# Loading the expert weights of a hybrid diffusion layer in blocks of 512 rows instead of 256

## The chip, the cores and the metric

One NeuronCore of a Trainium2 chip runs the whole program. The metric is the device time of one execution, in microseconds (us). TensorE (PE) multiplies, VectorE (DVE) and ScalarE (ACT) work element by element, GpSimd (POOL) here only sets buffers to zero and issues small transfers, and SyncE (SP) issues the weight transfers. Every transfer between HBM and the on-chip memory is spread over the core's 16 DMA engines.

## What is computed

One layer of a diffusion backbone runs on two groups of 128 tokens with 1024 features each, in float32: a modulated RMSNorm, a token mixer (attention, a gated recurrence and a gated MLP behind one input projection), an output projection, and then a mixture of experts in which each of the 256 tokens uses 4 of 32 experts. The part that the change touches is the last one:

```python
def swiglu_expert(xb, wg, bg, wu, bu, wd, bd):
    gate = jnp.minimum(xb @ wg + bg, SWIGLU_LIMIT)
    up = jnp.clip(xb @ wu + bu, -SWIGLU_LIMIT, SWIGLU_LIMIT)
    glu = gate * jax.nn.sigmoid(SWIGLU_ALPHA * gate)
    return ((up + 1.0) * glu) @ wd + bd

# routed_moe: logits = hf @ wr + br; gates = softmax of the top 4;
# out[token] += gate * swiglu_expert(hf[token]) for each of its 4 experts
```

Each expert has three 1024 x 1024 float32 matrices of 4 MB, so the 32 experts are 384 MB of weights, and every one of them is read once. The other weights are 41 MB.

## The kernel before

All weights pass through one buffer, `ring`, of 12 slots of 1 MB (8 KB in each of 128 partitions). SP issues one transfer for a slot, in a fixed order, one after another, with a counter `n`: 8 of `w_mod` (n = 0 to 7), 13 of `w_in`, 12 of `w_mod`, 4 of `w_out`, 4 of `w_mod`, and from n = `AT_MOE` = 41 on the 384 of the experts. Transfer n goes to slot n mod 12, and `slot_free` makes SP wait until PE has used up chunk n - 12. PE counts used chunks in the semaphore `chunks_used`, and waits for the semaphore of a slot (`slot_wait`) before it reads it.

The rows of the 1 MB differ in how they lie in HBM. A partition of a `w_mod` slot receives four separate runs of 2 KB, one of a `w_in` slot eight runs of 1 KB, one of a `w_out` slot two of 4 KB. An expert's chunk is 256 whole rows of a matrix; partition p takes rows 2p and 2p + 1, which are neighbours in HBM, so it is one run of 8 KB:

```python
return sp.dma_start(view.rearrange("p (k n) -> p k n", k=2),
                    w[0, bass.ds(e, 1), 256 * r:256 * (r + 1), :].rearrange("a (p k) n -> p (a k) n", p=P))
```

Since a partition holds two neighbouring rows of the matrix, the other operand has to be ordered in the same way. That is why DVE writes the normalised tokens in a permuted order of features (`pairs`, `rows_out_of`, line 951; the last step in line 959), why the router's weights `rw` are loaded with the same permutation, and why the activated products `ab` are written permuted (line 1038).

The order of PE's work in the expert stage is written out by hand (line 1524 on): the gate product of expert 0, then for each expert e the UP product, `combine` of expert e - 1 (its result is added to the tokens, line 1482), the GATE product of e + 1, the transposes of the activations of e (line 1495), the `gather` of the tokens of e + 2 (line 1447), the DOWN product of e, and the transposes of its gates (line 1502). A product is 4 chunks of 8 matmuls (line 1471), and after each chunk `chunks_used` rises by one. UP and GATE products begin with 4 matmuls for the bias (line 1466). The weights are loaded in the order GATE 0, UP 0, GATE 1, DOWN 0, UP 1, GATE 2, DOWN 1 and so on, to UP 31 and DOWN 31. Each group of 3 matrices for one expert is 12 chunks, a full ring.

Beside PE, DVE clips the gate product (line 1025) and the UP product (line 1033) and multiplies them (line 1038), and ACT copies tokens, transposed activations and results (lines 618, 626, 630). Loops for experts with more than 64 tokens follow; they are compiled in but are not entered with these inputs. The last step is a second RMSNorm and four output transfers.

Of the kernel before, what the change touches and what calls it, by code (L numbers as in the profile page):

```python
# [20 lines left out]
ALU = mybir.AluOpType  # L21
# [3 lines left out]
P = 128  # L25
# [33 lines left out]
AT_MOE = AT_MODG2 + 4  # L59
AT_END = AT_MOE + 12 * NE  # L60
WOUT = [2, 3, 0, 1]
# [39 lines left out]
def hybrid_layer(nc, x_prompt, x_sample, cache_k, cache_v, state_hgrn_fwd, state_hgrn_bwd, c, c_ctx,  # L101
# [6 lines left out]
    with ctx:  # L108
# [178 lines left out]
        def at_moe(m, e):  # L287


            return AT_MOE + 12 * e + {GATE: 0 if e == 0 else -4, UP: 4, DOWN: 12 if e + 1 < NE else 8}[m]  # L290

# [22 lines left out]
        def _(sp):  # L314
# [36 lines left out]
            def load_rows(view, w, e, r):  # L351
                return sp.dma_start(view.rearrange("p (k n) -> p k n", k=2),  # L352
                                    w[0, bass.ds(e, 1), 256 * r:256 * (r + 1), :].rearrange("a (p k) n -> p (a k) n", p=P))

            def load_matrix(m, e):
                nonlocal n
                assert n == at_moe(m, e)
                for r in range(4):
                    slot_free(n)
                    load_rows(ring[:, n % RING, :], (w_gate, w_up, w_down)[m], e, r).then_inc(slot_loaded[n % RING], 16)  # L360
                    n += 1
# [10 lines left out]
            with sp.If(n_over > 0):  # L372
                with sp.Fori(0, MAX_OVER) as j:
                    with sp.If(n_over > j):
                        e = sp.value_load(small_i[0:1, bass.ds(j, 1)], min_val=0, max_val=NE - 1)
                        sp.wait_ge(chunks_used, j * 12 + AT_END)
                        for cidx in range(12):
                            load_rows(ring[:, cidx, :], (w_gate, w_up, w_down)[cidx // 4], e, cidx % 4).then_inc(ev("over_loaded"), 16)

# [8 lines left out]
        def _(pool):  # L388
# [27 lines left out]
            small_load("mixer_loaded", ong, bcast_row(hgrn_onorm_g[0:1, :]))  # L416
            small_load("mixer_loaded", rw.rearrange("p (r k) e -> p r k e", r=4), router_w[0].rearrange("(r p k) e -> p r k e", p=P, k=2))
            small_load("mixer_loaded", rbias, router_b)
# [34 lines left out]
        def _(act):  # L453
# [182 lines left out]
            for e in range(NE):  # L636
                act_transposed(e)
                if e + 1 < NE:
                    sigmoid_step(e + 1)
                if e + 2 < NE:  # L640
                    tokens_out(e + 2, e % 2)
                rows_out(e, at_moe(DOWN, e) + 4)
            act.wait_ge(ev("over_list"), 1)
            n_over = act.value_load(small_i[0:1, 16:17], min_val=0, max_val=MAX_OVER)
            with act.If(n_over > 0):
                with act.Fori(0, MAX_OVER) as j:
                    with act.If(n_over > j):
                        tokens_out(j + NE, 0)
                        sigmoid_step(j + NE)
                        act_transposed(j + NE)  # L650
                        rows_out(j + NE, j * 12 + AT_END + 12)

# [11 lines left out]
        def _(dve):  # L664
# [266 lines left out]
            def pairs(ap):  # L931
                return ap.rearrange("p (r m k) -> p r m k", r=4, k=2)

            def rows_out_of(t):
                return rows[:, t, :].rearrange("p (r k m) -> p r m k", r=4, k=2)

# [16 lines left out]
            for t in range(2):  # L953
                dve.wait_ge(ev("rms2"), t + 1)
                ch.step(V.reciprocal(rs2[:, t:t + 1], rs2[:, t:t + 1]))
                dve.wait_ge(ev("rows_scaled"), t + 3)
                for r in range(4):
                    block_r = rows[:, t, 256 * r:256 * (r + 1)]
                    ins = V.scalar_tensor_tensor(block_r, block_r, rs2[:, t:t + 1],
                                                 shf[:, 256 * r:256 * (r + 1)].rearrange("p (m k) -> p k m", k=2), ALU.mult, ALU.add)  # L960
                ins.then_inc(ev("h2_ready"), 1)
# [69 lines left out]
            def up_step(count, done):  # L1031
                dve.wait_ge(chunks_used, done)
                V.tensor_scalar(upb, B[1], -LIMIT, LIMIT, ALU.max, ALU.min).then_inc(ev("up_clip"), 1)  # L1033
                dve.wait_ge(ev("glu_ready"), count + 1)
                dve.wait_ge(ev("up_clip"), count + 1)
                for r in range(2):
                    cols = slice(256 * r, 256 * (r + 1))
                    ins = V.scalar_tensor_tensor(ab[:, cols].rearrange("p (k m) -> p m k", k=2), upb[:, cols].rearrange("p (m k) -> p m k", k=2), 1.0,  # L1038
                                                 actb[:, cols].rearrange("p (m k) -> p m k", k=2), ALU.add, ALU.mult)
                ins.then_inc(ev("a_ready"), 1)  # L1040

# [14 lines left out]
            pick_tokens(1)  # L1056
            gate_step(0, at_moe(GATE, 0) + 4, later=False)
            for e in range(NE):
                if e + 2 < NE:
                    dve.wait_ge(ev("xe_ps"), e + 2)  # L1060
                    pick_tokens(e + 2)
                if e:
                    dve.wait_ge(ev("gT_ps"), e)
                pick_gates(e)
                glu_step(e)
                up_step(e, at_moe(UP, e) + 4)
                if e + 1 < NE:
                    gate_step(e + 1, at_moe(GATE, e + 1) + 4)
                gates_out(e)
            dve.wait_ge(ev("over_list"), 1)  # L1070
            n_over = dve.value_load(small_i[0:1, 16:17], min_val=0, max_val=MAX_OVER)
            with dve.If(n_over > 0):
                with dve.Fori(0, MAX_OVER) as j:
                    with dve.If(n_over > j):
# [13 lines left out]
                        ins.then_inc(ev("pg_ready"), 1)  # L1088
                        gate_step(j + NE, j * 12 + AT_END + 4)
                        glu_step(j + NE)  # L1090
                        up_step(j + NE, j * 12 + AT_END + 8)
                        gates_out(j + NE)
# [19 lines left out]
        def _(pe):  # L1112
# [338 lines left out]
            def main_rows(m, e, r):  # L1451

                n = at_moe(m, e) + r
                slot_wait(n)
                return ring[:, n % RING, :]

            def over_rows(m, e, r):
                return ring[:, 4 * m + r, :]

            def product(bank, m, e, lhsT, arrived, pick=None):  # L1460


                if m < 2:
                    row = ident[:, NE * (m + 1) + e:NE * (m + 1) + e + 1].to_broadcast([P, CAP]) if pick is None else pick
                    for half in range(2):
                        mm(bank[CAP * half:CAP * (half + 1), :], row, mbias[:, 512 * half:512 * (half + 1)], start=True, stop=False)  # L1466
                for r in range(4):
                    w = arrived(m, e, r).rearrange("p (k n) -> p k n", k=2)
                    for kk in range(2):
                        for half in range(2):  # L1470
                            ins = mm(bank[CAP * half:CAP * (half + 1), :], lhsT(2 * r + kk), w[:, kk, 512 * half:512 * (half + 1)],  # L1471
                                     start=m == 2 and r == 0 and kk == 0, stop=r == 3 and kk == 1)
                    ins.then_inc(chunks_used, 1)
# [74 lines left out]
            with pe.If(n_over > 0):  # L1548
                with pe.Fori(0, MAX_OVER) as j:
                    with pe.If(n_over > j):  # L1550
                        gather(j + NE)
                        pe.wait_ge(ev("xe_ready"), j + (NE + 1))
                        pe.wait_ge(ev("over_loaded"), j * 192 + 192)
                        product(B[0], GATE, 0, tokens(0), over_rows, over_pick[:, 0, :])
# [35 lines left out]
```

## Time and profile before

| | |
|---|---|
| median of 3 runs | 1229.23 us (1227.69 to 1230.12) |
| the profiled execution | 1229.05 us |
| its span, from the first to the last instruction | 1227.2 us |
| around the span | 1.85 us |
| PE busy | 1178.6 us, 96% of the span |
| DVE, ACT, POOL busy | 21%, 12%, 2% |
| moved by DMA | 456.00 MB, mean 372 GB/s |
| expert stage, from the first GATE product on | 264.5 us to 1212 us of the span |

A busy time of 96% says little here by itself, because matmuls are pipelined and an engine can be busy while it is late. What is to be read is which wait ends last in each part of the expert stage, and how fast the DMA engines move the weights there. All times below count from the start of the span.

### The profile page before, as it was taken

Reading aid. Unit: us, or ns where it says so; the run is one execution under the profiler, and the core shown is the slowest. Engines: PE = TensorE matmul, PEld = TensorE weight load, DVE = VectorE, ACT = ScalarE, POOL = GpSimd, SP = SyncE. Lnnn points to the kernel's source line nnn. Section 1 sums busy time; section 2 is a strip of 40 time slices with the busy share of each in tenths; the row PEclk is TensorE's granted clock in tenths of the full one; section 3 lists DMA queues with packets and bytes.
Section 4 is the critical chain, followed back from the end, with each engine's and each line's share of the span. In section 5 each row is a group of like instructions: output and inputs, shape, how many; then the busy total and the mean of one; then the engine's idle time right before and its main releaser. Section 6 shows DMA issues by size and latency. Waiting matters only on the chain.

```text
span 1227.2 us, 13618 instructions
## 1 busy us (share of the span) xinstructions
PE 1178.6 (96%) x5974; PEld 546.0 (44%) x5974; DVE 256.9 (21%) x567; ACT 142.9 (12%) x273; POOL 20.2 (2%) x39
## 2 busy tenths in 40 slices
PE   6599999999999999999999999999999999999995
PEld 1288975464444444444444444444443333333321
DVE  1325574421111111111111111111111111111113
ACT  1122423111000000000000100000000000000001
POOL 3100000000000000000000000000000000000000
PEclk9599999999999999999999999999999999999998
DMA  9993439639999999999999999999999999999993
GB/s 319 331 362 120 153 122 394 250 127 398 383 422 421 421 421 421 421 422 421 420 421 421 422 420 421 421 421 421 421 421 421 422 420 421 420 422 422 419 422 113
DMA packets 86051, 456.00 MB, mean 372 GB/s; under 512 B 7968, under 2 KB 21300, under 8 KB 36711
## 3 DMA queue, kind: packets, MB, share of 16 engines
q1 hardware_dynamic: 82928, 446.73, 90.1%
q0 software_dynamic: 2064, 6.98, 1.7%
q10 hardware_dynamic: 998, 1.40, 0.5%
q8 instruction: 48, 0.79, 0.3%
q14 instruction: 13, 0.10, 0.0%
HBM read 453.38 MB, written 1.70 MB: 371 GB/s over the span
## 4 chain that ended last, share of the span: by engine, by line
PE 60%; DMA 22%; DVE 2%; SPq 1%; issue 0%; ACT 0%; DVEq 0%
PE bank L1471 39%; DMA ring<-in_w_up 22%; PE bank L1447 7%; PE bank L1466 4%; PE bank L1482 4%; PE bank L1347 2%; PE bank L1495 1%; PE bank L1142 1%; PE bank L1502 1%; SPq L352 1%; PE bank L1174 0%; PE bank L1149 0%; PE bank L1415 0%; PE bank L1511 0%; PE bank L1383 0%
## 5 line engine op out<-in xcount | busy, mean ns | idle before, releaser
L1471 PE MATMUL bank<-ring,at_pool 128*64 128x512 f32 x2048 | 456.7, 595 | 5.6 <-DMA ring<-in_w_up 4.5
L1471 PEld LDWEIGHTS bank<-ring,at_pool 128*64 128x64 f32 x2048 | 145.7, 137 | 306.1 <-issue 270.3
L1471 PE MATMUL bank<-ring,k_pool 128*64 128x512 f32 x1024 | 227.5, 596 | 2.6 <-ACT k_pool L626 1.4
L1471 PEld LDWEIGHTS bank<-ring,k_pool 128*64 128x64 f32 x1024 | 70.3, 137 | 134.1 <-issue 125.0
L1447 PE MATMUL bank<-d_pool,rows 128*128 128x64 f32 x1024 | 118.0, 273 | 0.0
L1447 PEld LDWEIGHTS bank<-d_pool,rows 128*128 128x128 f32 x1024 | 116.9, 192 | 1.3 <-issue 1.3
L626 ACT COPY k_pool<-bank 128x512 f32<-128x512 f32 x32 | 18.7, 585 | 579.0 <-PE bank L1495 579.0
L1019 DVE COPY cumT<-bank 128x256 f32<-128x256 f32 x32 | 13.6, 424 | 346.2 <-PE bank L1502 346.2
L1025 DVE TENSOR_SCALAR k_pool<-bank 128x512 f32<-128x512 f32 x32 | 22.1, 691 | 256.5 <-PE bank L1471 256.5
L1466 PE MATMUL bank<-kv_pool,cst 128*64 128x512 f32 x256 | 69.4, 620 | 0.7 <-DVE small_i L1054 0.7
L1482 PE MATMUL bank<-d_pool,cumT 64*128 64x512 f32 x256 | 63.6, 615 | 0.6 <-DVE cumT L1019 0.6
L1033 DVE TENSOR_SCALAR k_pool<-bank 128x512 f32<-128x512 f32 x32 | 22.1, 691 | 199.7 <-PE bank L1471 199.7
L1192 PE MATMUL bank<-colsT,ring 128*128 128x256 f32 x224 | 52.2, 395 | 0.8 <-DVE colsT L729 0.8
L1192 PEld LDWEIGHTS bank<-colsT,ring 128*128 128x128 f32 x224 | 44.2, 199 | 8.1 <-DVE colsT L729 1.2
L1195 PE MATMUL bank<-ring,colsT 128*128 128x256 f32 x192 | 43.4, 380 | 0.0
L630 ACT COPY d_pool<-bank 128x512 f32<-128x512 f32 x32 | 18.7, 585 | 209.1 <-PE bank L1471 209.1
L1482 PEld LDWEIGHTS bank<-d_pool,cumT 64*128 64x128 f32 x256 | 22.1, 186 | 41.0 <-issue 40.2
L1142 PE MATMUL bank<-ring,condT 128*32 128x512 f32 x192 | 29.5, 749 | 10.6 <-DMA ring<-in_w_mod 10.6
L1195 PEld LDWEIGHTS bank<-ring,colsT 128*128 128x128 f32 x192 | 35.7, 190 | 4.6
L1038 DVE SCALAR_TENSOR_TENSOR kv_pool<-k_pool 128x256 f32<-128x256 f32 x64 | 33.9, 611 | 3.3
L618 ACT COPY at_pool<-bank 128x512 f32<-128x512 f32 x32 | 18.7, 585 | 91.4 <-PE bank L1447 91.4
L1347 PE MATMUL bank<-ring,colsT 128*128 128x512 f32 x64 | 27.9, 593 | 0.0
(295 smaller groups left out, 544.4 us busy)
## 6 DMA issues: line engine op xcount, KB each, us to landing
ring<-in_w_gate SPq DMA_DIRECT2D x128, 1024.0 KB, 20.5
ring<-in_w_up SPq DMA_DIRECT2D x128, 1024.0 KB, 21.4
ring<-in_w_down SPq DMA_DIRECT2D x128, 1024.0 KB, 20.7
ring<-in_w_mod SPq DMA_DIRECT2D x24, 1024.0 KB, 9.4
ring<-in_w_in SPq DMA_DIRECT2D x13, 1024.0 KB, 12.5
ring<-in_w_out SPq DMA_DIRECT2D x4, 1024.0 KB, 6.9
k_pool<-in_const_masks POOLq DMA_DIRECT2D x1, 1024.0 KB, 7.9
g<-in_b_mod POOLq DMA_DIRECT2D x2, 512.0 KB, 12.2
```

The source lines that it names most:

```text
L618: nc.scalar.copy(xe[:, buf].rearrange("p k s -> p (k s)"), B[3]).then_inc(ev("xe_ready"), 1)
L1025: V.tensor_scalar(actb, B[0], LIMIT, None, ALU.min).then_inc(ev("gate_min"), 1)
L1033: V.tensor_scalar(upb, B[1], -LIMIT, LIMIT, ALU.max, ALU.min).then_inc(ev("up_clip"), 1)
L1038: ins = V.scalar_tensor_tensor(ab[:, cols].rearrange("p (k m) -> p m k", k=2), upb[:, cols].rearrange("p (m k) -> p m k", k=2), 1.0, actb[ ...
L1142: ins = mm(B[mod_bank(n)][32 * j:32 * (j + 1), :], condT[:, 4 * r + j, :], w[:, j, :], start=r == 0, stop=r == 1, tile_position=(0, 32 * j))
L1192: ins = mm(bank[:, 256 * r:256 * (r + 1)], w[:, k, P * r:P * (r + 1)], hT[:, k, :, :], start=k == 0, stop=k == KT - 1)
L1195: ins = mm(bank[:, 256 * r:256 * (r + 1)], hT[:, k, r, :], w[:, k, :], start=k == 0, stop=k == KT - 1)
L1347: ins = mm(B[2 * t + half], catT[:, 2 * WOUT[i] + kk, t, :], w[:, kk, 512 * half:512 * (half + 1)], start=i == 0 and kk == 0, stop=i == 3 ...
L1447: ins = mm(B[3][:, CAP * k:CAP * (k + 1)], rows[:, t, P * k:P * (k + 1)], Ptok[:, t, :], start=t == 0, stop=t == 1)
L1466: mm(bank[CAP * half:CAP * (half + 1), :], row, mbias[:, 512 * half:512 * (half + 1)], start=True, stop=False)
L1471: ins = mm(bank[CAP * half:CAP * (half + 1), :], lhsT(2 * r + kk), w[:, kk, 512 * half:512 * (half + 1)], start=m == 2 and r == 0 and kk = ...
L1482: ins = mm(B[4 + 2 * t + half], gT[r, P * t:P * (t + 1)], ysb[r, :], start=False, stop=False)
```

## The change

A transfer now brings 512 rows of an expert's matrix (2 MB) into two neighbouring slots, and partition p takes rows 4p to 4p + 3, one run of 16 KB. The ring is used as `PAIRS` = 6 pairs of slots in this stage; the first pair is the one that `pair_of` gives for n = 41, which is slots 6 and 7. A product has 2 such chunks of 16 matmuls, and PE waits and counts once for each. SP waits for a pair as a whole: for the first six transfers until the last earlier chunk in either of its two slots is used, after that until the transfer six before is used. The permutations of the tokens, of the router's weights and of the activated products go from two to four neighbouring rows. In line 959 there are now 2 instructions over 512 columns for each token block where there were 4 over 256, and in line 1038 there is 1 over 512 for each expert where there were 2 over 256. Everything before n = 41 is loaded as it was.

```diff
+PAIRS = RING // 2
+AT_END = AT_MOE + 6 * NE
...
-            return AT_MOE + 12 * e + {GATE: 0 if e == 0 else -4, UP: 4, DOWN: 12 if e + 1 < NE else 8}[m]
+            return AT_MOE + 6 * e + {GATE: 0 if e == 0 else -2, UP: 2, DOWN: 6 if e + 1 < NE else 4}[m]
+
+        def pair_of(n):
+            return (n - AT_MOE + 3) % PAIRS
+
+        def pair_loaded(n):
+            return slot_loaded[2 * pair_of(n)]
+
+        def pair_loads(n):
+            before = len(range(2 * pair_of(n), AT_MOE, RING))
+            return 16 * (before + (n - AT_MOE) // PAIRS + 1)
+
+        def pair_rows(n):
+            return ring[:, 2 * pair_of(n):2 * pair_of(n) + 2, :].rearrange("p s w -> p (s w)")
...
             def load_rows(view, w, e, r):
-                return sp.dma_start(view.rearrange("p (k n) -> p k n", k=2),
-                                    w[0, bass.ds(e, 1), 256 * r:256 * (r + 1), :].rearrange("a (p k) n -> p (a k) n", p=P))
+                return sp.dma_start(view.rearrange("p (k n) -> p k n", k=4),
+                                    w[0, bass.ds(e, 1), 512 * r:512 * (r + 1), :].rearrange("a (p k) n -> p (a k) n", p=P))
...
-                for r in range(4):
-                    slot_free(n)
-                    load_rows(ring[:, n % RING, :], (w_gate, w_up, w_down)[m], e, r).then_inc(slot_loaded[n % RING], 16)
+                for r in range(2):
+                    if n < AT_MOE + PAIRS:
+                        sp.wait_ge(chunks_used, min(AT_MOE, 32 + 2 * (n - AT_MOE)))
+                    else:
+                        sp.wait_ge(chunks_used, n - PAIRS + 1)
+                    load_rows(pair_rows(n), (w_gate, w_up, w_down)[m], e, r).then_inc(pair_loaded(n), 16)
                     n += 1
...
-            small_load("mixer_loaded", rw.rearrange("p (r k) e -> p r k e", r=4), router_w[0].rearrange("(r p k) e -> p r k e", p=P, k=2))
+            small_load("mixer_loaded", rw.rearrange("p (r k) e -> p r k e", r=2), router_w[0].rearrange("(r p k) e -> p r k e", p=P, k=4))
...
-                rows_out(e, at_moe(DOWN, e) + 4)
+                rows_out(e, at_moe(DOWN, e) + 2)
...
             def pairs(ap):
-                return ap.rearrange("p (r m k) -> p r m k", r=4, k=2)
+                return ap.rearrange("p (r m k) -> p r m k", r=2, k=4)
...
-                for r in range(4):
-                    block_r = rows[:, t, 256 * r:256 * (r + 1)]
+                for r in range(2):
+                    block_r = rows[:, t, 512 * r:512 * (r + 1)]
                     ins = V.scalar_tensor_tensor(block_r, block_r, rs2[:, t:t + 1],
-                                                 shf[:, 256 * r:256 * (r + 1)].rearrange("p (m k) -> p k m", k=2), ALU.mult, ALU.add)
+                                                 shf[:, 512 * r:512 * (r + 1)].rearrange("p (m k) -> p k m", k=4), ALU.mult, ALU.add)
...
-                for r in range(2):
-                    cols = slice(256 * r, 256 * (r + 1))
-                    ins = V.scalar_tensor_tensor(ab[:, cols].rearrange("p (k m) -> p m k", k=2), upb[:, cols].rearrange("p (m k) -> p m k", k=2), 1.0,
-                                                 actb[:, cols].rearrange("p (m k) -> p m k", k=2), ALU.add, ALU.mult)
-                ins.then_inc(ev("a_ready"), 1)
+                V.scalar_tensor_tensor(ab.rearrange("p (k m) -> p m k", k=4), upb.rearrange("p (m k) -> p m k", k=4), 1.0,
+                                       actb.rearrange("p (m k) -> p m k", k=4), ALU.add, ALU.mult).then_inc(ev("a_ready"), 1)
...
                 n = at_moe(m, e) + r
-                slot_wait(n)
-                return ring[:, n % RING, :]
+                pe.wait_ge(pair_loaded(n), pair_loads(n))
+                return pair_rows(n)
...
-                for r in range(4):
-                    w = arrived(m, e, r).rearrange("p (k n) -> p k n", k=2)
-                    for kk in range(2):
+                for r in range(2):
+                    w = arrived(m, e, r).rearrange("p (k n) -> p k n", k=4)
+                    for kk in range(4):
                         for half in range(2):
...
                     ins.then_inc(chunks_used, 1)
```

## Rows read from the trace of the kernel before

**Rows 1.** Page, part 2: GB/s in 40 equal slices of the span.

```profile
GB/s 319 331 362 120 153 122 394 250 127 398 383 422 421 421 421 421 421 422 421 420 421 421 422 420 421 421 421 421 421 421 421 422 420 421 420 422 422 419 422 113
```

**Rows 2.** Windows: us, busy of PE, PEld, DVE, ACT, POOL, clock, DMA share, GB/s.

```profile
252.00:256.00 4.00, 3.94 (x17) 2.08 (x16) 2.98 (x13) 0.00 (x0) 0.00 (x0) 1.00 0.00 0
...
330.00:340.00 10.00, 10.00 (x50) 3.31 (x48) 1.86 (x6) 0.58 (x1) 0.00 (x0) 1.00 0.95 366
340.00:350.00 10.00, 10.00 (x48) 3.23 (x46) 1.75 (x3) 0.00 (x0) 0.00 (x0) 1.00 1.01 425
...
336.00:890.00 554.00, 554.00 (x2852) 230.43 (x2850) 81.69 (x190) 43.41 (x76) 0.00 (x0) 1.00 1.01 421
890.00:1190.00 300.00, 293.52 (x1472) 115.34 (x1470) 42.72 (x98) 22.35 (x40) 0.00 (x0) 1.00 1.01 421
```

**Rows 3.** Chain that ended last, in order of time: start us, us, what.

```profile
277.62 6.87 PE bank L1471 x32
...
308.34 6.87 PE bank L1471 x32
315.20 1.92 PE bank L1482 x8
...
869.24 1.92 PE bank L1482 x8
...
899.61 26.72 DMA ring<-in_w_up
...
1170.02 27.81 DMA ring<-in_w_up
1197.87 1.94 PE bank L1471 x8
1199.81 1.92 PE bank L1482 x8
```

**Rows 4.** PE's timeline, expert stage: start us, us, line, operation, [idle before].

```profile
926.37 1.94 PE L1471 MATMUL bank<-ring,at_pool 128*64 128x512 f32 x8 [0.27 <-DMA ring<-in_w_up]
...
1203.11 7.09 PE L1471 MATMUL bank<-ring,k_pool 128*64 128x512 f32 x32 [0.68 <-ACT k_pool L626]
```

**Rows 5.** DMA view, 400 to 500 us: packets and how many are small.

```profile
DMA packets 5779, 42.12 MB, mean 421 GB/s; under 512 B 642, under 2 KB 642, under 8 KB 642
```

**Rows 6.** DMA view, 0 to 30 us: GB/s in 40 slices of 0.75 us.

```profile
GB/s 0 0 86 247 291 339 388 396 418 300 224 259 251 254 262 251 251 246 271 265 317 353 366 388 385 374 388 388 390 388 393 388 374 404 410 431 434 434 333 396
```

**Rows 7.** DMA view, 30 to 60 us: GB/s in 40 slices of 0.75 us.

```profile
GB/s 339 320 249 210 197 235 180 213 352 322 309 344 262 385 404 391 414 377 362 352 352 347 350 344 350 350 350 347 350 344 348 358 347 358 351 348 350 348 351 348
```

**Rows 8.** Instructions that write `ring`, on SP's queue: duration ns min/median/max.

```profile
L321 SPq DMA_DIRECT2D ring<-in_w_mod x24: 367/368/6599, 1.5 to 192.4; - x24
L321 SPq DMA_DIRECT2D ring<-in_w_in x13: 2823/2922/13437, 22.0 to 75.6; - x13
```

**Rows 9.** Windows of 40 to 80 us and of the last weight transfers; columns as above.

```profile
40.00:80.00 40.00, 32.83 (x129) 24.16 (x130) 10.71 (x24) 6.70 (x10) 2.84 (x4) 0.72 1.09 357
...
1206.00:1208.00 2.00, 2.00 (x12) 0.70 (x10) 0.00 (x0) 0.00 (x0) 0.00 (x0) 1.00 0.05 20
```

**Rows 10.** SP's timeline around the stage's start: start us, us, line, operation.

```profile
235.27 2.90 SPq L352 DMA_DIRECT2D ring<-in_w_gate  x4
267.77 5.48 SPq L352 DMA_DIRECT2D ring<-in_w_down  x4
```

**Rows 11.** Timeline of the edited DVE instructions, one of PE behind them.

```profile
237.71 0.69 DVE L946 TENSOR_TENSOR xres<-xres,tmp 128x512 f32<-128x512 f32 x1
...
240.49 1.67 DVE L959 SCALAR_TENSOR_TENSOR rows<-rows,small,shf 128x256 f32<-128x256 f32 x4
...
242.21 1.09 PE L1408 MATMUL bank<-cst,rows 128*128 128x128 f32 x8 [0.91 <-DVE rows L959]
```

**Rows 12.** DVE's timeline at the last expert.

```profile
1199.86 0.69 DVE L1033 TENSOR_SCALAR k_pool<-bank 128x512 f32<-128x512 f32 x1 [8.05 <-PE bank L1471]
1200.66 1.06 DVE L1038 SCALAR_TENSOR_TENSOR kv_pool<-k_pool 128x256 f32<-128x256 f32 x2
```

More of the change, by code:

```diff
@@ L59 @@
 AT_MOE = AT_MODG2 + 4
-AT_END = AT_MOE + 12 * NE
+PAIRS = RING // 2
+AT_END = AT_MOE + 6 * NE
 WOUT = [2, 3, 0, 1]
@@ L375, in _ @@
                         e = sp.value_load(small_i[0:1, bass.ds(j, 1)], min_val=0, max_val=NE - 1)
-                        sp.wait_ge(chunks_used, j * 12 + AT_END)
-                        for cidx in range(12):
-                            load_rows(ring[:, cidx, :], (w_gate, w_up, w_down)[cidx // 4], e, cidx % 4).then_inc(ev("over_loaded"), 16)
+                        sp.wait_ge(chunks_used, j * 6 + AT_END)
+                        for cidx in range(6):
+                            load_rows(pair_rows(AT_MOE + cidx), (w_gate, w_up, w_down)[cidx // 2], e, cidx % 2).then_inc(ev("over_loaded"), 16)
             for t in range(2):
@@ L650, in _ @@
                         act_transposed(j + NE)
-                        rows_out(j + NE, j * 12 + AT_END + 12)
+                        rows_out(j + NE, j * 6 + AT_END + 6)
             nc.scalar.activation(rsf[:, 0:1], eps, ACT.Sqrt).then_inc(ev("root_table"), 1)
@@ L931, in pairs @@
             def pairs(ap):
-                return ap.rearrange("p (r m k) -> p r m k", r=4, k=2)
+                return ap.rearrange("p (r m k) -> p r m k", r=2, k=4)
             def rows_out_of(t):
-                return rows[:, t, :].rearrange("p (r k m) -> p r m k", r=4, k=2)
+                return rows[:, t, :].rearrange("p (r k m) -> p r m k", r=2, k=4)
             dve.wait_ge(ev("caches_stored"), 48)
@@ L1056, in _ @@
             pick_tokens(1)
-            gate_step(0, at_moe(GATE, 0) + 4, later=False)
+            gate_step(0, at_moe(GATE, 0) + 2, later=False)
             for e in range(NE):
@@ L1065, in _ @@
                 glu_step(e)
-                up_step(e, at_moe(UP, e) + 4)
+                up_step(e, at_moe(UP, e) + 2)
                 if e + 1 < NE:
-                    gate_step(e + 1, at_moe(GATE, e + 1) + 4)
+                    gate_step(e + 1, at_moe(GATE, e + 1) + 2)
                 gates_out(e)
@@ L1088, in _ @@
                         ins.then_inc(ev("pg_ready"), 1)
-                        gate_step(j + NE, j * 12 + AT_END + 4)
+                        gate_step(j + NE, j * 6 + AT_END + 2)
                         glu_step(j + NE)
-                        up_step(j + NE, j * 12 + AT_END + 8)
+                        up_step(j + NE, j * 6 + AT_END + 4)
                         gates_out(j + NE)
@@ L1453, in main_rows @@
                 n = at_moe(m, e) + r
-                slot_wait(n)
-                return ring[:, n % RING, :]
+                pe.wait_ge(pair_loaded(n), pair_loads(n))
+                return pair_rows(n)
             def over_rows(m, e, r):
-                return ring[:, 4 * m + r, :]
+                return pair_rows(AT_MOE + 2 * m + r)
             def product(bank, m, e, lhsT, arrived, pick=None):
@@ L1466, in product @@
                         mm(bank[CAP * half:CAP * (half + 1), :], row, mbias[:, 512 * half:512 * (half + 1)], start=True, stop=False)
-                for r in range(4):
-                    w = arrived(m, e, r).rearrange("p (k n) -> p k n", k=2)
-                    for kk in range(2):
+                for r in range(2):
+                    w = arrived(m, e, r).rearrange("p (k n) -> p k n", k=4)
+                    for kk in range(4):
                         for half in range(2):
-                            ins = mm(bank[CAP * half:CAP * (half + 1), :], lhsT(2 * r + kk), w[:, kk, 512 * half:512 * (half + 1)],
-                                     start=m == 2 and r == 0 and kk == 0, stop=r == 3 and kk == 1)
+                            ins = mm(bank[CAP * half:CAP * (half + 1), :], lhsT(4 * r + kk), w[:, kk, 512 * half:512 * (half + 1)],
+                                     start=m == 2 and r == 0 and kk == 0, stop=r == 1 and kk == 3)
                     ins.then_inc(chunks_used, 1)
@@ L1552, in _ @@
                         pe.wait_ge(ev("xe_ready"), j + (NE + 1))
-                        pe.wait_ge(ev("over_loaded"), j * 192 + 192)
+                        pe.wait_ge(ev("over_loaded"), j * 96 + 96)
                         product(B[0], GATE, 0, tokens(0), over_rows, over_pick[:, 0, :])
```

## The prediction

> **What bounds the kernel now.** I began with the page's slices of the span [rows 1]: from about 335 us to 1196 us the DMA engines move 419 to 422 GB/s without a gap, while PE is listed as busy all the time. Two resources are near their limit in this stretch, so the next view was the chain that ended last. Up to 891 us it holds PE's work alone, and `combine` (L1482) comes back exactly every 29.16 us: 315.20, 344.36 and 19 periods after the first, 869.24 [rows 3]. That is PE's own time for one expert. From 899.61 on the chain is a loop: a slot is freed, SP issues, the transfer lands 26 to 28 us later, PE uses it. The last one lands at 1197.83, and `combine` of expert 30 starts at 1199.81 [rows 3]. With PE's period it would start at 315.20 + 30 x 29.16 = 1190.00. So PE loses 9.8 us to the weights, all of it after 890 us, where the windows show its busy time fall to 293.5 of 300 us [rows 2].
>
> The two rates explain when. One expert is 12 transfers of 1,048,576 bytes; at 421 GB/s that is 12 x 2.491 = 29.89 us, or 0.73 us more than PE's 29.16. The full ring at the start is a lead that is eaten up by 0.73 us an expert and is gone after some 20 experts. The DMA engines rest for the last time near 335 us: the window 330 to 340 moves 366 GB/s, the next 425 [rows 2]. From there to the landing at 1197.83 are 344 transfers (those that refill the slots from DOWN 1 on, up to the last of UP 31): 344 x 2.491 = 857 us, which fits. The slowest of the 16 engines is a little slower: between the landings just before 926.37 [rows 4] and at 1197.83 lie 9 experts, 108 transfers, 2.514 us each. I anchor the sum at that landing and change only the time of a transfer.
>
> **What a longer run is worth.** This trace has three lengths of run with the queue full. In 1 MB each of the 16 engines moves 65,536 bytes, and the packet counts show the rest: 642 packets under 512 B in 42.12 MB [rows 5], which is 16 for each transfer, one for each engine. So 1 MB costs an engine 8 packets of 8 KB and one small one, 32 and one for `w_mod` (2 KB), 64 and one for `w_in` (1 KB).
> - 1 KB: the last 20 slices from 45 to 60 us have 344 to 358, mean 349.6 GB/s [rows 7]: 2.999 us for 1 MB, 65 packets.
> - 2 KB: six slices from 19.5 to 24 us have 388 to 393, mean 389 GB/s [rows 6]: 2.695 us, 33 packets.
> - 8 KB: 421 GB/s [rows 2]: 2.491 us, 9 packets.
>
> From 2 KB to 8 KB a packet costs 0.204 / 24 = 8.5 ns beside its bytes, from 1 KB to 8 KB 0.508 / 56 = 9.1 ns. The 1 KB point is the weaker one, since SP takes 2.92 us to issue one such transfer [rows 8] and could itself set the rate; but the DMA share is 1.09 then [rows 9], so the engines had a packet in hand all the time, and the 2 KB transfers, issued in 0.37 us, give nearly the same price. After the change 2 MB cost 8 packets of 16 KB and one small one, so 1 MB costs 4.5 packets instead of 9. I estimate a saving of 4.5 x 8.5 = 0.038 us to 4.5 x 9.1 = 0.041 us for 1 MB: 2.450 to 2.453 us, 427.5 to 428 GB/s. No row shows 16 KB, so the lower end for the saving is 0 (a run is no cheaper than two halves of it). I take 0.038 to 0.041, since three lengths lie on one line.
>
> The Trainium skill, "DMA: Bandwidth & Descriptors", § Why small descriptors are slow, gives about 3 cycles of overhead for each packet, which at the 850 MHz of its § Where 436 GB/s comes from would be an estimated 3.5 ns. The rows show 8.5 to 9.1 ns, and the measurement decides. By the page's figure the saving would be 0.016 us for 1 MB, and the time about 1226.5 us by the sum below.
>
> **What the pairs cost.**
> - Start. The ring is full and DMA idle (0 GB/s at 252 to 256 us [rows 2]) before the first GATE product. The first refill is issued when one chunk is used, at 267.77 [rows 10]; after the change when 16 matmuls are done, not 8. The same holds at the release that ends the last rest near 335 us. The 32 matmuls of UP 1 take 6.87 us [rows 3], so 8 take 1.72 us, and every later landing is 1.72 us later. The first six pairs themselves are in time: the last one waits for the last chunk of `w_mod`, as the last of the 1 MB transfers did (235.27 to 238.2 us [rows 10]), and 6 MB still to come then take 15 us, to about 252; UP 0 begins at 277.62 [rows 3].
> - End of a product. PE can start the last half of UP 31 only when all of it is there. In the schedule without waits UP 31 starts at 308.34 + 30 x 29.16 = 1183.14 [rows 3], and its second pair is needed 3.44 us later, at 1186.6.
> - The second pair of DOWN 31 lands before 1208 now [rows 9], and moves like that of UP 31, to about 1196. It is needed 3.5 us after DOWN 31 starts, which is 1203.11 - 9.8 = 1193.3 [rows 4], so at 1196.8.
> - SP issues 192 transfers instead of 384, each a matter of tenths of a us (0.37 for `w_mod`'s [rows 8]). The next transfer is issued while four pairs are still on the way, so this hides on both sides.
>
> **DVE's edits.** L959 becomes 2 instructions of 512 columns for each block; four of 256 take 1.67 us [rows 11], and a two-input one of 512 takes 0.69 [rows 11], so about 1.38: -0.3 us, and PE waited for it (0.91 us idle before L1408). The longer stride could take this away; bounds -0.6 to +0.3. L951 has the same elements: 0. L1038 goes from 1.06 us in two [rows 12] to between 0.69 and 1.2 in one: 0, since `combine` (1.92) and a GATE product (6.87) cover it, and at expert 31 `combine` alone covers the 1.86 us from the start of L1033 to the end of L1038; uncovered it costs at most 0.1 us, once.
>
> **The sum.** Write d for the saving for 1 MB. The last pair of UP 31 lands at 1197.83 + 1.72 - 344 d. With d = 0.038 to 0.041 that is 1186.5 to 1185.4, against 1186.6 needed: PE hardly waits, and its own period becomes the bound for the whole stage. The time is then 1229.05 (the profiled execution; the median of the runs is 0.18 higher) - 9.8 (all waits for weights gone) - 0.3 (L959) + 0.6. The last term is for short waits near the end, where the lead is about zero; the rows allow 0 to 2. That is **1219.5 us**, and 1218.3 to 1222 for this case.
>
> In general the time is 1219.0 + max(0, 13.0 - 344 d), where 13.0 is 1197.83 + 1.72 - 1186.6. It equals that of before at d = 0.0086, which is 422.5 GB/s.
>
> **The rivals.**
> - The rate rises, but less, to about 425 GB/s, the best that a 10 us window shows now (340 to 350 us [rows 2]). Then d = 0.0235, 13.0 - 8.1 = 4.9, about 1224 us; with prices of a packet down to half of mine, 1222 to 1227. For it: 425 may be where something behind the engines stops them. Against it: the fit gives 2.409 to 2.414 us for 65,536 bytes with no packets at all, so nothing shows up to 434 GB/s. In the Trainium skill, "HBM Reference", § Specifications (TRN2) puts a core that streams alone at about 425 GB/s, held by its 16 DMA engines, which would be this case. By the 3.5 ns of the page cited above the time falls into this case as well. No row here tells whether that is an end. Chance 0.12.
> - The time of before at 8 KB is a price of bytes, not of packets, or a run of 16 KB goes out as two packets of 8 KB. Then the ring in pairs only costs. With d = 0 the loop after 890 us begins some five experts earlier, its last landing is 1.72 us later and PE has 16 matmuls left behind it instead of 8: 1219.0 + 13.0 = 1232.0 us, slower. With two packets for a run only the small packet is saved, d = 0.004 and 1230.5. It decides below 422.5 GB/s. For it: `w_in` and `w_mod` also differ in how their rows lie in HBM, not only in the length of the run. Against it: they lie on one line with 8 KB. Chance 0.15.
> - Landing in pairs makes PE wait where it doesn't now, before 890 us, because the slowest engine's share of 2 MB comes later still. A wait of 0.5 us an expert would give 1235 us. Against it: the first pair of UP 1 takes the place of UP 0's, is issued near 277.62 + 3.44 = 281.1 us and needed at 308.34 [rows 3], so the lead is over 15 us there. Chance 0.05.
>
> **How the numbers follow.** My forecast has 0.68. It and the 425 GB/s case hold 0.80, so the range is 1217.8 to 1227.5: below, the floor of 1219.0 less the spread of the runs and the better end of L959. A measurement of this kernel tells 0.2% (2.5 us) from no change. Faster by more than that: all of 0.68 and 0.10 of the 425 case, 0.78. Within it: 0.02 of that case and 0.06 of the one with the rate unchanged. Slower: 0.14.
>
> **What would show it.** Slices at 427 to 428 GB/s after 340 us, packets over 8 KB halved; `combine` every 29.16 us up to expert 30, which would start near 1190; PE's waits for `ring` in the last 300 us near zero instead of 6.5 us; the first refill issued near 269.5 us; L1408 0.3 us earlier. The prediction is wrong if the rate stays under 425, or if PE's period itself grows.

## The result, and the profile after

The changed kernel takes 1218.47 us (median of 4 runs, 1216.95 to 1220.17); the kernel before, run beside it, 1228.46. The ratio is 0.9918 (95% interval 0.9899 to 0.9937): faster by 0.8%. The prediction was 1219.5 us. The profiled execution took 1216.95 us, with a span of 1214.8. "Line" numbers move by 10 to 22 in the new file: L1490 is the product that was L1471, L1501 `combine`, L981 was L959, L1058 was L1038, L1466 `gather`.

The page's slices in GB/s, where [rows 1] has 419 to 422 from the twelfth on:

```profile
GB/s 314 334 361 134 152 109 354 250 172 405 383 416 428 429 428 427 428 427 427 428 427 428 428 427 428 427 426 429 428 426 428 427 428 427 426 429 427 427 427 88
```

The windows, for [rows 2], and the packets of 400 to 500 us, for [rows 5]:

```profile
336.00:890.00 554.00, 554.00 (x2852) 230.45 (x2850) 81.65 (x171) 43.43 (x76) 0.00 (x0) 1.00 1.01 427
890.00:1190.00 300.00, 297.18 (x1508) 120.24 (x1504) 44.08 (x88) 22.27 (x39) 0.00 (x0) 1.00 1.00 424
```

```profile
DMA packets 2934, 42.72 MB, mean 427 GB/s; under 512 B 326, under 2 KB 326, under 8 KB 326
```

The rate is 427 GB/s where it was 421, and there are 2608 large packets in 42.72 MB, so they are 16 KB each. 326 small ones are 16 for each of some 20 transfers of 2 MB. From 890 to 1190 us PE is busy for 297.2 of the 300 us, where it was busy for 293.5.

The chain that ended last, for [rows 3]: start us, us, what.

```profile
312.71 1.92 PE bank L1501 x8
...
895.91 1.92 PE bank L1501 x8
...
1158.41 25.25 DMA ring<-in_w_up
1183.67 0.04 issue
1183.71 3.65 PE bank L1490 x16
1187.37 1.92 PE bank L1501 x8
```

`combine` comes every 29.16 us, now past 890 us too: (895.91 - 312.71) / 20 = 29.16. Transfers stand only at the very end, in front of the last half of UP 31. PE's timeline of the last two experts, for [rows 4], shows what is left:

```profile
1169.43 3.65 PE L1490 MATMUL bank<-ring,k_pool 128*64 128x512 f32 x16 [0.67 <-ACT k_pool L648]
1173.92 3.65 PE L1490 MATMUL bank<-ring,k_pool 128*64 128x512 f32 x16 [0.84 <-DMA ring<-in_w_down]
...
1178.81 3.65 PE L1490 MATMUL bank<-ring,at_pool 128*64 128x512 f32 x16
1183.71 3.65 PE L1490 MATMUL bank<-ring,at_pool 128*64 128x512 f32 x16 [1.25 <-DMA ring<-in_w_up]
```

Without a wait the second half of DOWN starts 3.51 us after the first (half of the 7.02 us from one step to the next where DOWN isn't held up) and that of UP 3.44 us (as the prediction has it). DOWN 30 and UP 31 have 1173.92 - 1169.43 = 4.49 and 1183.71 - 1178.81 = 4.90 us there, so they are 1.0 and 1.5 us late.

The time before the expert stage varies from one execution to the next by more than what is to be told apart here: the first GATE product starts at 263.34 us in this trace and at 260.35 in another one of the same kernel. So beside the times I use the length of the stage, from the first matmul of GATE 0 to the start of the last `combine`, for each trace. It is 1211.17 - 264.47 = 946.7 us before and 1198.72 - 263.34 = 935.4 us after. From the trace of before:

```profile
264.47 8.43 PE L1471 MATMUL bank<-ring,at_pool 128*64 128x512 f32 x32
...
315.13 1.99 PE L1482 MATMUL bank<-d_pool,cumT 64*128 64x512 f32 x8
...
1211.17 1.99 PE L1482 MATMUL bank<-d_pool,cumT 64*128 64x512 f32 x8 [0.61 <-DVE cumT L1019]
```

From the trace after:

```profile
263.34 7.07 PE L1490 MATMUL bank<-ring,at_pool 128*64 128x512 f32 x32
...
312.64 1.99 PE L1501 MATMUL bank<-d_pool,cumT 64*128 64x512 f32 x8
...
1198.72 1.99 PE L1501 MATMUL bank<-d_pool,cumT 64*128 64x512 f32 x8 [0.61 <-DVE cumT L1041]
```

In this trace GATE 0 takes 7.07 us at a granted clock of 1.00 (the upper of TensorE's two levels, 2.4 GHz), and the first `combine` starts 312.64 - 263.34 = 49.30 us after GATE 0. In the trace of before GATE 0 took 8.43 us, the mean granted clock of 262 to 276 us was 0.88 (so it stood at the lower level, 1.2 GHz, for a part of that time), and the first `combine` started 50.66 us after GATE 0. So 1.4 of its 946.7 us are the lower clock, and 945.3 are left. Below, a stage "at full clock" is the measured stage less what the first `combine` comes later than 49.30 us.

All three traces with runs of 8 KB (before and two below) lose 1.4 to 2.5 us in this way, and so do four of the nine others. That this belongs to the execution and not to the change is therefore likely but not shown. The mean granted clock of the executions on record lies between 0.979 and 0.987 for the kernel before and for the changed one alike.

### The profile page after: what moved, and what is told of

Its sections match the earlier page's. It is cut to its first block, busy times and chain, and to the rows that moved or that the text cites. A ratio compares the mean times of both kernels' runs of the same rounds, so it can differ in the third digit from the quotient of the medians.

```text
span 1214.8 us, 13390 instructions
## 1 busy us (share of the span) xinstructions
PE 1170.0 (96%) x5974; PEld 547.4 (45%) x5974; DVE 257.9 (21%) x531; ACT 142.9 (12%) x273; POOL 20.1 (2%) x39
## 4 chain that ended last, share of the span: by engine, by line
PE 81%; DMA 2%; DVE 2%; issue 0%; ACT 0%; DVEq 0%
PE bank L1490 53%; PE bank L1466 9%; PE bank L1485 5%; PE bank L1501 5%; DMA ring<-in_w_up 2%; PE bank L1366 2%; PE bank L1514 2%; PE bank L1161 1%; PE bank L1521 1%; PE bank L1193 0%; PE bank L1168 0%; PE bank L1434 0%; PE bank L1530 0%; PE bank L1402 0%; DVE xres L968 0%
## 5 line engine op out<-in xcount | busy, mean ns | idle before, releaser
L1490 PE MATMUL bank<-ring,at_pool 128*64 128x512 f32 x2048 | 450.6, 592 | 1.3 <-DMA ring<-in_w_up 1.3
L1490 PEld LDWEIGHTS bank<-ring,at_pool 128*64 128x64 f32 x2048 | 147.4, 137 | 293.6 <-issue 289.9
L1490 PE MATMUL bank<-ring,k_pool 128*64 128x512 f32 x1024 | 227.0, 595 | 2.2 <-ACT k_pool L648 1.3
L1490 PEld LDWEIGHTS bank<-ring,k_pool 128*64 128x64 f32 x1024 | 70.6, 137 | 132.9 <-issue 127.1
L1466 PE MATMUL bank<-d_pool,rows 128*128 128x64 f32 x1024 | 118.0, 273 | 0.0
L1466 PEld LDWEIGHTS bank<-d_pool,rows 128*128 128x128 f32 x1024 | 116.9, 192 | 1.3 <-issue 1.3
L1501 PE MATMUL bank<-d_pool,cumT 64*128 64x512 f32 x256 | 63.6, 615 | 0.6 <-DVE cumT L1041 0.6
L1501 PEld LDWEIGHTS bank<-d_pool,cumT 64*128 64x128 f32 x256 | 22.1, 186 | 41.0 <-issue 40.2
L1161 PE MATMUL bank<-ring,condT 128*32 128x512 f32 x192 | 28.4, 726 | 11.3 <-DMA ring<-in_w_mod 11.3
L1058 DVE SCALAR_TENSOR_TENSOR kv_pool<-k_pool 128x512 f32<-128x512 f32 x32 | 33.7, 1053 | 3.3
```

Of the source, the lines that this page charges most:

```text
L1058: V.scalar_tensor_tensor(ab.rearrange("p (k m) -> p m k", k=4), upb.rearrange("p (m k) -> p m k", k=4), 1.0, actb.rearrange("p (m k) -> p ...
L1161: ins = mm(B[mod_bank(n)][32 * j:32 * (j + 1), :], condT[:, 4 * r + j, :], w[:, j, :], start=r == 0, stop=r == 1, tile_position=(0, 32 * j))
L1466: ins = mm(B[3][:, CAP * k:CAP * (k + 1)], rows[:, t, P * k:P * (k + 1)], Ptok[:, t, :], start=t == 0, stop=t == 1)
L1490: ins = mm(bank[CAP * half:CAP * (half + 1), :], lhsT(4 * r + kk), w[:, kk, 512 * half:512 * (half + 1)], start=m == 2 and r == 0 and kk = ...
L1501: ins = mm(B[4 + 2 * t + half], gT[r, P * t:P * (t + 1)], ysb[r, :], start=False, stop=False)
```

## The experiments

The theory: an engine pays 8 to 10 ns for each packet beside its bytes, and longer runs mean fewer packets; with 427 GB/s the weights fall behind PE by so little that the lead of the full ring lasts nearly to the end. The rivals: the gain comes with the size of the transfer (its issue, landing and semaphore), or with the coarser waiting and counting; or the rate does not matter and PE alone decides.

**Pairs alone.** Two transfers of 1 MB with 8 KB runs fill a pair; tokens and activations are ordered as before.

```diff
+                rows = 256 * (2 * r + half)
+                return sp.dma_start(view[:, SLOT * half:SLOT * (half + 1)].rearrange("p (k n) -> p k n", k=2),
+                                    w[0, bass.ds(e, 1), rows:rows + 256, :].rearrange("a (p k) n -> p (a k) n", p=P))
```

> The ring in pairs alone: each pair is filled by two transfers of 1 MB with runs of 8 KB, as before the change, and PE waits for both. Price of a packet (a run): the expert stage stays at 421 GB/s, the pairs cost a later first refill and 16 matmuls behind the last landing, and the time is 1230 to 1233 us, slower than before by 2 to 4. Rival, the gain comes from the coarser counting and waiting and not from the run: 1217 to 1221 us, as with the change. Second rival, the pairs cost nothing: 1228 to 1229 us.

Measured: 1226.02 us, ratio 0.9999 (0.9969 to 1.0028), 421 GB/s. The time is below the expected range, and by it the pairs could cost nothing. But the stage of this trace begins at 258.67 us, 5.8 us before that of the trace of before, in code that is the same but for the first expert loads. The stage itself takes 1208.07 - 258.67 = 949.4 us; 2.5 of them are the lower clock, in GATE 0 and again in UP 1. At full clock it is 946.9 us, 1.6 longer than before, where the sum had 3.2 (13.0 us of waits with pairs at the old rate, less the 9.8 of before). The coarser counting brings nothing and costs a little.

**2 MB in runs of 8 KB.** One transfer for a pair, two blocks of 256 rows.

```diff
+                return sp.dma_start(view.rearrange("p (b k n) -> p b k n", b=2, k=2),
+                                    w[0, bass.ds(e, 1), 512 * r:512 * (r + 1), :].rearrange("a (b p k) n -> p (a b) k n", p=P, k=2))
```

> One transfer of 2 MB for a pair, but with two runs of 8 KB a partition, 256 rows apart in the matrix; tokens and activations ordered as before the change. Price of a packet: 1 MB needs 8 packets and half a small one, so 2.487 us where it was 2.491, 421 to 422 GB/s, and 1228 to 1232 us. Rival, price of a transfer (its issue, its landing, its semaphore): 426 to 428 GB/s and 1217 to 1221 us, as with the change.

Measured: 1230.79 us, ratio 1.0028 (1.0002 to 1.0054), 421 GB/s, a stage of 1212.75 - 264.42 = 948.3 us, 947.0 at full clock: 1.6 longer than before, like the run above. The packets of 400 to 500 us:

```profile
DMA packets 5458, 42.11 MB, mean 421 GB/s; under 512 B 322, under 2 KB 322, under 8 KB 322
```

The transfers are halved (322 small packets, not 642 as in [rows 5]), the 8 KB packets are as many as before, and the rate is that of before. The size of the transfer is not what pays.

**1 MB in runs of 16 KB, by halves of the partitions.**

```diff
+                rows = 512 * r + 256 * half
+                return sp.dma_start(view[HALF * half:HALF * (half + 1), :].rearrange("p (k n) -> p k n", k=4),
+                                    w[0, bass.ds(e, 1), rows:rows + 256, :].rearrange("a (p k) n -> p (a k) n", p=HALF))
```

> Runs of 16 KB in transfers of 1 MB: a pair is filled by two transfers of 64 partitions each, PE waits for both. Price of a packet: 1 MB needs 4 packets and one small one for each engine, 2.453 to 2.460 us, 426 to 427.5 GB/s, and 1217 to 1222 us. Rival, price of a transfer: 421 GB/s and 1229 to 1233 us.

Both expectations missed: 1736 us (1666 to 1845, 4 runs), ratio 1.3662 (1.358 to 1.3744). The trace is that of the 1845 us execution; it has 217 GB/s at 400 to 500 us and 213 to 301 in the windows of 100 us from 270 to 1770 us.

```profile
400.00:500.00 100.00, 63.88 (x250) 20.92 (x249) 7.89 (x17) 3.46 (x6) 0.00 (x0) 0.83 1.01 217
```

The DMA share is 1.01: the engines are never without a packet, but each packet of 16 KB takes twice as long, 1.2 us (16 engines for 100 us by 1325 packets) instead of 0.6. So this run does not tell the run's length from the transfer's size. The next one keeps the 64 partitions and the 1 MB, and spreads the partitions.

**1 MB in runs of 16 KB, by even and odd partitions.**

```diff
+                return sp.dma_start(view[half::2, :].rearrange("p (k n) -> p k n", k=4),
+                                    w[0, bass.ds(e, 1), 512 * r:512 * (r + 1), :].rearrange("a (p h k) n -> h p (a k) n", p=HALF, h=2)[half])
```

> As the run with 1 MB transfers of 64 neighbouring partitions and runs of 16 KB, which moved only 217 to 300 GB/s, but one transfer of a pair now takes the even partitions and the other the odd ones. If that run was slow because one half of the partitions takes only half of the writes that all 128 take: 426 to 427.5 GB/s, and 1217 to 1222 us, which would also show the run's length apart from the transfer's size. If a transfer of 64 partitions is slow in itself: 210 to 310 GB/s and 1600 to 1850 us again.

Measured: 1219.46 us, ratio 0.9928 (0.9894 to 0.9961), 427 GB/s, a stage of 1195.41 - 260.64 = 934.8 us, at full clock, where the change has 935.4.

```profile
DMA packets 3260, 42.74 MB, mean 427 GB/s; under 512 B 651, under 2 KB 651, under 8 KB 651
```

There are as many transfers as before the change, and the rate is that of the change. Together with the run of 2 MB in runs of 8 KB, this shows that the rate comes from the length of the run and not from the size of the transfer.

**Runs of 4 KB and of 32 KB.** The first changes one word of the load; the second makes three groups of four slots, with one transfer, one wait and one count for a matrix.

```diff
-                                    w[0, bass.ds(e, 1), 512 * r:512 * (r + 1), :].rearrange("a (p k) n -> p (a k) n", p=P))
+                                    w[0, bass.ds(e, 1), 512 * r:512 * (r + 1), :].rearrange("a (k p) n -> p (a k) n", p=P))
```

> The changed kernel with runs of 4 KB: a pair is still filled by one transfer of 2 MB, but partition p takes rows p, 128 + p, 256 + p and 384 + p of the 512, so the experts multiply rows in another order than the tokens' features and give other numbers. Price of a packet (8 to 9 ns beside its bytes, fitted from runs of 1, 2, 8 and 16 KB): 16.5 packets for 1 MB, 2.55 to 2.56 us, 410 to 411 GB/s, and 1249 to 1256 us. Rival, the length of a run costs nothing and something else of the change brought the rate: 421 GB/s or more, at most 1232 us.

```diff
+                return sp.dma_start(view.rearrange("p (k n) -> p k n", k=8),
+                                    w[0, bass.ds(e, 1), :, :].rearrange("a (p k) n -> p (a k) n", p=P))
...
+            return (n - AT_MOE + 2) % GROUPS
```

> One transfer for a whole matrix: 4 MB, runs of 32 KB, the ring as three groups of four slots, one wait and one count for 32 matmuls. Partition p takes rows 8p to 8p + 7, while the tokens' features stay ordered for four rows, so the experts give other numbers. Price of a packet: 2.25 packets for 1 MB, 2.43 to 2.44 us, 430 to 431.5 GB/s; the first refill and the last landing cost three and three chunks of 1.72 us more than in the kernel before, so the time is 1219 to 1224 us, slower than the change in spite of the faster transfers. Rival, the gain ends at 16 KB: 427 GB/s and 1225 to 1230 us.

Measured with 4 KB: 1255.68 us, ratio 1.0223 (1.0185 to 1.0261), 409 GB/s, a stage of 976.9 us, 974.5 at full clock. With 32 KB: 1218.68 us, 0.3 below the expected range and not slower than the change, ratio 0.9927 (0.9901 to 0.9954), 431 GB/s, a stage of 937.8 us. 2.3 of these are the lower clock, in GATE 0 (7.69 us) and in UP 1 (8.03 us instead of 7.04, with a mean granted clock of 0.66 from 300 to 305 us). At full clock the stage is 935.4 us, as with the change. The windows of 400 to 500 us of both:

```profile
400.00:500.00 100.00, 100.00 (x510) 40.61 (x507) 14.99 (x30) 6.86 (x12) 0.00 (x0) 1.00 1.03 409
```

```profile
400.00:500.00 100.00, 100.00 (x526) 43.15 (x528) 13.58 (x28) 8.52 (x15) 0.00 (x0) 1.00 1.00 431
```

With 16.5, 9, 4.5 and 2.25 packets for 1 MB an engine takes 2.564, 2.491, 2.456 and 2.433 us (1,048,576 bytes by 409, 421, 427, 431 GB/s): 9.7, 7.8 and 10 ns for a packet from one to the next, each difference good to about 1 or 2 ns, since the rates are rounded to 1 GB/s. The line goes on past 16 KB, but the stage gains nothing by it: PE still waits 1.8 us for DOWN 30 and 1.2 us for UP 31. That the later refills of 4 MB at a time eat up the gain is the likely reason; it was not tried apart.

**Half of the bytes.** What PE needs when weights are always early.

```diff
-                return sp.dma_start(view.rearrange("p (k n) -> p k n", k=4),
-                                    w[0, bass.ds(e, 1), 512 * r:512 * (r + 1), :].rearrange("a (p k) n -> p (a k) n", p=P))
+                return sp.dma_start(view.rearrange("p (k n) -> p k n", k=4)[:, 0:2, :],
+                                    w[0, bass.ds(e, 1), 512 * r:512 * (r + 1), :].rearrange("a (p k) n -> p (a k) n", p=P)[:, 0:2, :])
```

> The changed kernel with half of the expert weights: each transfer brings only the first two of the four rows of a partition (1 MB), and the other two hold what the ring held before, so the experts' results are of other numbers; the instructions of all engines are the same. The weights are then always early, and the time is PE's own. If the last experts still wait for weights after the change (about 2.5 us in its trace): 1215 to 1217 us, 1.5 to 3.5 below the changed kernel. If PE's period was already the bound of the whole stage, as the prediction has it: the same as the changed kernel within 1 us, 1217.5 to 1219.5.

Measured: 1214.08 us, 0.9 below the lower expected range, ratio 0.9896 (0.987 to 0.9922), a stage of 1194.55 - 261.81 = 932.7 us at full clock, 2.6 shorter than with the change. The weights still bind after the change, in the last two experts.

**A seventh buffer.** `PAIRS` is 7 here; the edit in parts:

```diff
+        late = sb("late", 4 * D)
+        gsc, shf, colsT = late[:, 0:D], late[:, D:2 * D], late[:, 2 * D:4 * D]
...
+            i = (n - AT_MOE) % PAIRS
+            return (i + 3) % 6 if i < 6 else 6
...
+                    if n == AT_MOE + 6:
+                        sp.wait_ge(ev("logits_ps"), 1)
```

> The changed kernel with a seventh buffer of 2 MB: gsc, shf and colsT lie side by side, are no longer needed once the router's logits are made, and take the seventh transfer and then every seventh. If the last experts wait because the lead of the full ring has been eaten up, 5 us more of it take these waits away: 1213 to 1216.5 us, like the run with half of the bytes (1214). If the waits come from the rate at the end, whatever the lead: 1217 to 1220 us, as with the change.

> The changed kernel once more, beside the seventh buffer on the same chip. 1217 to 1220 us; its own spread tells how much of a difference of 2 to 4 us can be told.

> The seventh buffer once more, for the interval: 1212 to 1217 us, with PE's waits for weights in the last 300 us under 0.5 us in total.

Measured: the seventh buffer 1213.57 us (1212.25 to 1217.35, 6 runs), ratio 0.9892 (0.9867 to 0.9917); the changed kernel beside it 1217.47 (1212.62 to 1222.07, 7 runs), ratio 0.9927 (0.9900 to 0.9954); the seventh buffer again 1214.04 (1210.77 to 1219.0, 6 runs), ratio 0.9899 (0.9871 to 0.9926). In neither of its two traces does PE wait for a weight at the end; from the second:

```profile
261.83 7.06 PE L1494 MATMUL bank<-ring,at_pool 128*64 128x512 f32 x32
...
1167.90 7.09 PE L1494 MATMUL bank<-ring,k_pool 128*64 128x512 f32 x32 [0.68 <-ACT k_pool L652]
...
1194.58 1.99 PE L1505 MATMUL bank<-d_pool,cumT 64*128 64x512 f32 x8 [0.61 <-DVE cumT L1045]
```

The stage is 932.7 us, that of the run with half of the bytes. The first trace has 935.1 us, 2.3 of them at the lower clock, so 932.7 at full clock too. The second trace of the changed kernel has 936.8 us. Its clock fell in the last half of UP 31, behind a wait of 2.27 us for weights: these 16 matmuls took 5.26 us where they take 3.65, at a mean granted clock of 0.72 from 1180 to 1186 us. Without that it is 935.2, against 935.4 in the first. So by the stage the seventh buffer brings 2.5 to 2.7 us, and its cause is seen: the waits of the last two experts are gone.

By whole times the interval of each run of it overlaps that of the changed kernel. All 12 executions together have a mean of 1214.6 us and the 11 of the changed kernel one of 1218.2, a difference of 3.5 us (95% interval 1.2 to 5.9). This version is faster than both kernels.

## Why the prediction was right, step by step

- **The price of a packet** was right in kind and in size. 427.5 to 428 GB/s were forecast, 427 are there. By these rates 1 MB is cheaper by 0.035 us; the forecast had 0.038 to 0.041. Run length and transfer size, which the change moves together, were told apart by two runs that moved one each. The rival with the rate unchanged and the one that stops at 425 fall: 431 GB/s were seen with 32 KB. So does the rival with a cheaper packet: no step of the line is below 7.8 ns. The Trainium skill, "DMA: Bandwidth & Descriptors", § Why small descriptors are slow, gives about 3 cycles, which the prediction turns into an estimated 3.5 ns; the 7.8 to 10 ns of the runs differ, and the measurement decides.
- **What the pairs cost** was mis-sized by half. The sum has 13.0 - 9.8 = 3.2 us; the two runs with pairs and 8 KB runs have stages that are 1.6 us longer than before. The later refill came as forecast. In the run with 2 MB, whose GATE 0 had the clock of before, the first refill was issued at 269.45 us (269.5 forecast), and the one at DOWN 1 at 332.69, where before it was 331.01. The 16 matmuls behind the last landing came too. But the last pair of UP 31 did not land 1.72 us later: counted from the first `combine`, PE could begin on it after 882.6 us in both runs, where before it began on the last 1 MB of UP 31 after 882.7. Why is open. Half a small packet less for 1 MB makes some 1.4 us of this in the run with 2 MB, but nothing in the other.
- **The landing** of the last pair of UP 31 was forecast for 1185.4 to 1186.5; it landed at 1183.67, in a stage that began 1.1 us earlier and lost 1.4 us less in GATE 0. On the old footing that is 1186.2. That is inside the forecast partly by luck: with the measured 0.035 us for 1 MB the sum gives 1187.5, and the landing is earlier than that by the unexplained part of the pairs' cost.
- **The step "all waits for weights gone, 9.8 us"** was mis-sized, and with it the claim that PE's own period becomes the bound for the whole stage. I put `combine` of expert 30 at 30 periods after the first. But expert 30 has no `gather` in front of its DOWN product (there is no expert 32), so PE would be there 3.5 us earlier, less 0.67 us in which the transposed activations are then waited for. In the run with half of the bytes the last period, from `combine` of expert 29 to that of 30, is 1183.14 - 1156.75 = 26.39 us and not 29.16. Without waits the stage takes 932.7 us, 14.0 less than before; 1.4 of that is the clock in GATE 0, and 12.6 are waits, not 9.8. The term "+0.6, short waits near the end" should have been 2.6. The two errors nearly cancel, because the landing, not PE, ends the stage: -9.8 + 0.6 against -12.6 + 2.6. So it is luck that `combine` of expert 30 came where it was forecast, near 1190: it started at 1187.37, on the old footing 1189.9, but the landing put it there, not PE's period. The 1219.0 us of the general formula are no floor either: with the seventh buffer, where PE waits for no weights at the end, the medians are 1213.6 and 1214.0 us.
- **L959** was forecast at -0.3 us with bounds of -0.6 to +0.3, and is +0.5: four instructions took 1.67 us [rows 11], two now take 2.17, and PE waits 1.39 us for them, not 0.91.

```profile
239.19 2.17 DVE L981 SCALAR_TENSOR_TENSOR rows<-rows,small,shf 128x512 f32<-128x512 f32 x2
...
241.41 1.09 PE L1427 MATMUL bank<-cst,rows 128*128 128x128 f32 x8 [1.39 <-DVE rows L981]
```

  I took the price from an instruction whose operands are contiguous. PE starts L1427 earlier than in [rows 11] all the same, since all of this trace runs 1.3 us earlier by then. L1058 takes 1.053 us, as its two halves did, and hides as forecast.
- **The new waits before 890 us**, the third rival, did not come: there PE is busy for all of 554 us.

Of the 12.1 us between the two profiled executions 11.3 lie in the stage: 12.6 of waits less the 2.6 that are left, and 1.4 of clock. 1.1 lie before the stage, and 0.3 are lost again around the span (2.15 us, where it was 1.85); why was not tried. The medians differ by 10.0 us.

## What to carry to other kernels

Fit the cost of a transfer from the lengths of run that the trace already has; here three lengths gave the rate of a fourth within 0.3%. That the size of the transfer does not matter is not seen from the fit; it took two runs that each changed one of the two. Then ask by how much the transfers are behind the engine, and how long the lead lasts: in this kernel a gain in rate was worth something only where the lead ran out, and a buffer that was dead in that stage made the lead long enough to take away the last 2.6 us of waits. When the period of a loop is carried to its last rounds, check what those rounds leave out.

## What the runs showed of the hardware

- Transfers to 64 neighbouring partitions moved 217 GB/s at 400 to 500 us even though the other half's transfer was behind each in the queue; those to 64 even or odd partitions moved 427. The rows in HBM are not the cause: the pairs of 1 MB with 8 KB runs read the same 256 neighbouring rows in one transfer at 421. The Trainium skill, "SBUF — State Buffer", § Door 1, has partitions 0 to 63 on 8 of 16 ports, for about 218 GB/s, and this window of the trace agrees. Later windows of that trace have up to 301 GB/s; why it varies was not tried. The Trainium skill, "SBUF — State Buffer", § "Can I just issue two DMAs to hit both halves?" says that the only way to reach all 16 ports is one transfer spanning all 128 partitions. The run with 64 alternate partitions, at 427 GB/s, shows that such a transfer need not fill all 128, and there the measurement decides.
- DVE's two-input instruction L959 with a read at a step of 2 floats took 479 ns for 256 columns (median of 8), and L981 with a step of 4 floats 1140 ns for 512 (median of 4). That the step of 4 is the cause was not tried apart.
- The DMA engines do not keep step. Before the change the landings from 926.37 to 1197.83 us came 2.514 us apart for 1 MB, while the mean rate of that stretch, 421 GB/s, makes 2.491. When no more transfers follow, the rate falls in steps, from 418 GB/s at 1195 to 1198 us over 303, 238, 209 and 135 (2 us each) to 20 at 1206 to 1208. So some engines end their share up to 10 us before the last; which ones and why is open.
